# A hybrid decoder step: 48 instead of 32 prompt units inside the sample loop, all scores of the next unit first, and SyncE as the one issuer of value transfers

## What is computed

```python
mod = silu(c) @ w_ada + b_ada                  # (9, 6144): shift, scale, gate, twice; one row per sequence
h = x * (1 + scale1) + shift1
qa, ka, va, qb, kb, vb = split(h @ w_in)       # 6 column groups of 512; rope on the q and k groups
# mixer A: 8 heads of 64; keys at distance 0..128, 0..512 by 4, 0..2048 by 16, three softmaxes mixed
# mixer B: 4 heads, two q/k maps each: (softmax(q1 k1) - lambda softmax(q2 k2)) v, then an RMS norm
x = layer_norm(alpha * x + gate1 * (concat(oa, ob) @ w_o))
x = layer_norm(alpha * x + gate2 * conv_ffn(x * (1 + scale2) + shift2))
# outputs also: the samples' key and value windows moved on by 8 rows (HBM to HBM copies, 4080 KB each, 16 of them)
```

## Time and profile before

| | |
|---|---|
| median of three runs | 1229.12 us (1226.54 to 1235.38) |
| profiled run: its own time | 1233.46 us |
| profiled run: span | 1231.5 us |
| busy in the span: PE, DVE, POOL, ACT | 1052.7, 839.2, 357.9, 269.5 us |
| bytes moved by the DMA queues | 276.54 MB, mean 225 GB/s |

### The profile page before, as it was taken

The page is one execution under the profiler, slowest core; times in us unless marked ns, Lnnn a source line. Parts: engine busy times, 40 slices in busy tenths (PEclk is TensorE's granted clock), DMA queues, the critical chain, the costliest instruction groups (busy, mean ns, idle before and its releaser), DMA issues.

```text
span 1231.5 us, 23995 instructions
## 1 busy us (share of the span) xinstructions
PE 1052.7 (85%) x9389; PEld 854.0 (69%) x9389; DVE 839.2 (68%) x1513; ACT 269.5 (22%) x580; POOL 357.9 (29%) x379
## 2 busy tenths in 40 slices
PE   5599999999578677677776996999999999999994
PEld 3377777666455555455555775999999999677772
DVE  1657457167676767667659467567676687998958
ACT  0310010132132223322242104332233222100002
POOL 2333233100000000000016005456565665433323
PEclk9699999999888889778786997999999999999997
DMA  8959895596899999999990215475567731413102
GB/s 303 399 171 327 300 353 174 187 331 220 279 351 344 316 367 322 360 313 343 333 322 1 64 53 195 143 265 207 205 244 274 264 105 69 149 58 106 70 17 77
DMA packets 112549, 276.54 MB, mean 225 GB/s; under 512 B 9608, under 2 KB 33174, under 8 KB 108837
## 3 DMA queue, kind: packets, MB, share of 16 engines
q1 hardware_dynamic: 99125, 250.82, 58.6%
q10 hardware_dynamic: 13312, 24.19, 5.5%
HBM read 264.60 MB, written 76.69 MB: 277 GB/s over the span
## 4 chain that ended last, share of the span: by engine, by line
PE 60%; DVE 18%; DMA 7%; SPq 7%; issue 4%; POOL 2%; ACT 2%; ACTq 0%; DVEq 0%; POOLq 0%; PEldq 0%
PE wide L1576 16%; PE wide L1578 15%; PE wide L1577 15%; DVE ring L1151 3%; PE wide L1650 2%; DMA ring<-in_cache_k 2%; DMA ring<-in_w_ada 2%; PE wide L1639 2%; PE wide L1701 2%; PE wide L1732 2%; DVE ring_r L1083 2%; SPq L598 2%; SPq L433 1%; PE wide L1525 1%; DMA ring<-in_w_down 1%
## 5 line engine op out<-in xcount | busy, mean ns | idle before, releaser
L747 POOL TENSOR_TENSOR ring_r<-ring,ring_r 128x1024 fp32r<-128x1024 f32 x70 | 184.9, 2650 | 271.4 <-DVE ring_r L1043 204.5
L1576 PE MATMUL wide<-x_sb_r,ring_r 128*128 128x288 f32 x704 | 211.4, 300 | 8.2 <-DVE ht_r L1065 5.1
L1577 PE MATMUL wide<-ht_r,ring_r 128*128 128x288 f32 x704 | 209.3, 297 | 0.0
L1578 PE MATMUL wide<-x_sb_r,ring_r 128*128 128x288 f32 x704 | 208.7, 296 | 0.0
L1578 PE MATMUL wide<-ring_r,ht_r 128*128 128x512 f32 (+1 forms) x400 | 158.2, 395 | 0.0
L1151 DVE STREAM_TRANSPOSE ring<-ring 128x512 f32<-128x512 f32 x208 | 129.2, 673 | 20.8 <-DMA ring<-in_cache_k 19.0
L1576 PEld LDWEIGHTS wide<-x_sb_r,ring_r 128*128 128x128 f32 x704 | 133.3, 189 | 11.7 <-issue 11.2
L1578 PEld LDWEIGHTS wide<-x_sb_r,ring_r 128*128 128x128 f32 x704 | 134.2, 191 | 0.0
L1577 PEld LDWEIGHTS wide<-ht_r,ring_r 128*128 128x128 f32 x704 | 133.8, 190 | 0.0
L1576 PE MATMUL wide<-ring_r,x_sb_r 128*128 128x512 f32 (+1 forms) x240 | 97.0, 404 | 10.5 <-DVE ht_r L1065 8.5
L1701 PE MATMUL wide<-ring,x_sb 128*32 128x128 f32 (+1 forms) x1792 | 69.3, 305 | 40.4 <-DVE ring L1151 40.3
(11 more groups left out here) (226 smaller groups left out, 1900.0 us busy)
## 6 DMA issues: line engine op xcount, KB each, us to landing
ring<-in_cache_k SPq DMA_DIRECT2D x128, 256.0 KB
out_wks<-in_cache_win_k SPq DMA_DIRECT2D x8, 4080.0 KB, 19.0
out_wvs<-in_cache_win_v SPq DMA_DIRECT2D x8, 4080.0 KB, 25.3
ring<-in_w_ada SPq DMA_DIRECT2D x12, 2048.0 KB, 10.0
ring<-in_w_up SPq DMA_DIRECT2D x22, 1024.0 KB, 7.6
ring<-in_cache_win_k SPq DMA_DIRECT2D x16, 1024.0 KB
ring<-in_w_in SPq DMA_DIRECT2D x6, 2048.0 KB, 18.4
room<-in_cache_v ACTq DMA_DIRECT2D x32, 256.0 KB
```

The costliest lines, as they stand in the source:

```text
L747: nc.gpsimd.tensor_tensor(rest, w, high.bitcast(F32), ALU.subtract).then_inc(wl_rest, 1)
L1576: nc.tensor.matmul(out, left[0], right[0], start=first, stop=False)
L1577: nc.tensor.matmul(out, left[0], right[1], start=False, stop=False)
L1578: return nc.tensor.matmul(out, left[1], right[0], start=False, stop=last)
```

## The change

- **Modulation moved.** `ada` 4 to 11 leave the prompt stage. They run between the projection units, at the units in `LATE_UNIT`, through one 2 MB buffer of their own (`late`), loaded one ahead by SP (`load_late`), which waits until the chunk before has been multiplied.
- **Window copies** of the first four samples are issued one at a time after the units in `COPY_UNIT`, not in pairs.
- **Prompt units.** `NU` is 16: heads 0 to 3 of mixer A stay in the prompt stage, the other 48 units go into the sample loop, three per step (`PER = 3`, `prompt_step`).
- **Queries** lie packed two heads to a tile (`qt`) rather than padded with zeros (`qtp`): the 4 MB memset on POOL goes, ACT copies each tile with one instruction instead of two, and the score product contracts 64 rows instead of 128.
- **Order on PE in a step.** All groups of step `w + 1` are scored first, then its new rows (into bank 7, not 4), then all groups of step `w` are weighed.
- **Issuing.** `values_by_act` is always false: SP issues all value groups, in the order keys (w, 0), keys (w, 1), values (w-1, 0), keys (w, 2), values (w-1, 1), keys (w, 3), values (w-1, 2 and 3), new keys of w, new values of w-1. ACT issues only mixer A's key tails (`load_key_tail`), behind its exponentials of the step.
- Buffers are laid out anew; new keys and new values have one buffer each instead of two.

The core of the diff:

```diff
+LATE_UNIT = {4: 3, 5: 6, 6: 10, 7: 13, 8: 16, 9: 20, 10: 23, 11: 26}
+COPY_UNIT = {1: (0, "k"), 4: (0, "v"), 8: (1, "k"), 11: (1, "v"), 14: (2, "k"), 18: (2, "v"), 21: (3, "k"), 24: (3, "v")}
...
-        NU = 32
+        NU = 16
         pb = pa[NU:]
+        PER = len(pb) // (2 * DB)
...
         def values_by_act(w, g):
-            return w < len(sa) and w > 0 and (g < 2 if sa[w][0] else g == 1)
+            return False
+        def load_key_tail(eng, w):
+            G = NG[w] + 2
+            ks = G % NK
+            if G >= NK:
+                eng.wait_ge(kg_t, G - NK + 1)
+            win_k = flat_k[0][sa[w][1]].rearrange("(g r) h d -> g r (h d)", r=16)
+            for i in range(4):
+                eng.dma_start(kraw[ks][32 * i:32 * i + 32, 0:2, :], win_k[96:128, 8 + i:16:4, :]).then_inc(kg_in[ks], 16)
...
+            def load_late(ch):
+                if ch > 4:
+                    sp.wait_ge(ada_mm, ch)
+                src = a["w_ada"][0].rearrange("(k p) n -> p k n", p=P)
+                sp.dma_start(late, src[:, :, CH * ch:CH * ch + CH]).then_inc(late_in, 16)
...
+            load_keys(0, 0)
+            load_keys(0, 1)
+            sp.wait_ge(w_used, CHUNK_AT[("in", 5)] + 1)
+            sp.wait_ge(ada_mm, 12)
+            load_key_tail(sp, 0)
+            for w in range(1, len(sa) + 1):
+                here = len(groups[sa[w][0]]) if w < len(sa) else 0
+                if here:
+                    load_keys(w, 0)
+                    load_keys(w, 1)
+                load_values(sp, w - 1, 0)
+                if here == 4:
+                    load_keys(w, 2)
+                load_values(sp, w - 1, 1)
+                if here == 4:
+                    load_keys(w, 3)
+                for g in range(2, len(groups[sa[w - 1][0]])):
+                    load_values(sp, w - 1, g)
+                if here:
+                    sp.wait_ge(kn_t, w)
+                    load_new_keys(sp, w)
                 if w >= 2:
-                    sp.wait_ge(kn_t, w - 1)
                     sp.wait_ge(sa_pv, w - 1)
-                    load_new(sp, w)
+                    load_new_values(sp, w - 1)
...
+                if w + 1 < len(sa) and sa[w + 1][0] == 0:
+                    load_key_tail(act, w + 1)
...
-                for g in range(4):
-                    if g < len(nxt):
-                        score_group(w + 1, g)
-                    if g == 0:
-                        pe.wait_ge(sa_pt, 2 * w + 2)
-                        pe.wait_ge(sa_ph, w + 1)
-                    if g < len(groups[m]):
-                        weigh_group(w, g)
-                    if g == 2:
-                        turn_b(2 * w)
-                        scores_b(2 * w + 1)
+                for g in range(len(nxt)):
+                    score_group(w + 1, g)
+                    if g == 1:
+                        prompt_step(PER * w + 1)
+                if nxt:
+                    score_new(w + 1)
+                else:
+                    prompt_step(PER * w + 1)
+                pe.wait_ge(sa_pt, 2 * w + 2)
+                pe.wait_ge(sa_ph, w + 1)
+                for g in range(len(groups[m])):
+                    weigh_group(w, g)
+                    if g == 1:
+                        if nxt:
+                            pe.wait_ge(sa_min, w + 2)
+                        prompt_step(PER * w + 2)
```

More of the change, by code:

```diff
@@ L144, in build, with mod_s @@
         lam4 = part(room, 3584, 256).rearrange("p (n d) -> p n d", n=4)
[L146 to L150, removed]
+        mod_early = ht[:, :, :].rearrange("p k t -> p (k t)")[:, 6 * NT:6 * NT + 2 * CH].rearrange("p (b n) -> p b n", b=2)
+        mod_late = mix[:, 2048:2048 + 2 * CH].rearrange("p (b n) -> p b n", b=2)
+        def mod_s(ch):
+            return (mod_early if ch < 4 else mod_late)[:, ch % 2, :]
+        late = part(room, 12288, KT_D * CH).rearrange("p (k n) -> p k n", k=KT_D)
+        qt = part(room, 0, 4096).rearrange("p (f t) -> p f t", f=8)
+        kt = part(room, 4096, 4096).rearrange("p (f t) -> p f t", f=8)
+        vp = part(room, 8192, 4096).rearrange("p (m t d) -> p t m d", t=TP, m=2)
         tmp_a = part(room, 16384, 1024).rearrange("p (b n) -> p b n", b=2)
@@ L276, in build @@
         vg_in = [sem(f"v_group_loaded_{i}") for i in range(NV)]
-        new_in = [sem(f"new_rows_loaded_{i}") for i in range(2)]
+        kn_in, vn_in = sem("new_keys_loaded"), sem("new_values_loaded")
         new_zero, qbd_zero = sem("new_zeroed"), sem("queries_zeroed")
@@ L560, in _ @@
                 if t == TP:
[L561 to L565, removed]
-            sp.wait_ge(page_in, 16)
[L569 to L601, removed]
@@ new lines, in _, with load_keys @@
+                    if s < 4:
+                        load_chunk(6 + s)
+                for ch, at in LATE_UNIT.items():
+                    if at == n and ch < 11:
+                        load_late(ch + 1)
+                if n in COPY_UNIT:
+                    i, which = COPY_UNIT[n]
+                    move_window(i, (("cache_win_k", "wks") if which == "k" else ("cache_win_v", "wvs"),))
+            sp.wait_ge(page_in, 16)
+            sp.wait_ge(w_used, CHUNK_AT[("in", 4)] + 1)
+            def load_keys(w, g):
+                m, b = sa[w]
+                G = NG[w] + g
+                ks = G % NK
+                if G >= NK:
+                    sp.wait_ge(kg_t, G - NK + 1)
+                if m == 0:
+                    win_k = flat_k[0][b].rearrange("(g r) h d -> g r (h d)", r=16)
+                    sp.dma_start(kraw[ks][:, :, :], win_k[:, 4 * g:4 * g + 4, :]).then_inc(kg_in[ks], 64)
+                else:
+                    for t, pg in enumerate(page_numbers(sp, b, g)):
+                        sp.dma_start(kraw[ks][:, t, :], flat_k[1][bass.ds(pg, 1)].rearrange("a p h d -> (a p) (h d)"))\
+                            .then_inc(kg_in[ks], 16)
@@ L721, in _ @@
             pool.wait_ge(w_used, CHUNK_AT[("in", 5)] + 1)
+            for i, place in enumerate((kn, ktn)):
+                nc.gpsimd.memset(place, 0.0).then_inc(new_zero, 1)
+                pool.wait_ge(new_zero, i + 2)
             nc.gpsimd.memset(qbd, 0.0).then_inc(qbd_zero, 1)
@@ L731, in _ @@
                 last.then_inc(q_bd, 1)
[L732 to L737, removed]
             def rest_of_piece(q):
@@ L1106, in _ @@
             jobs += [(5 * c - 1.4, "split", c) for c in range(1, 6)]
+            jobs += [(n - 0.5, "late_rows", ch) for ch, n in LATE_UNIT.items()]
+            jobs += [(n + 0.55, "late_sum", ch) for ch, n in LATE_UNIT.items()]
             dve.wait_ge(rope_in, 16)
             for _, what, n in sorted(jobs):
+                if what == "late_rows":
+                    ada_rows(n)
+                    continue
+                if what == "late_sum":
+                    ada_sum(n)
+                    continue
                 if what == "split":
@@ L1517, in ada_rows @@
             def ada_rows(ch):
-                n = CHUNK_AT[("ada", ch)]
-                landed(n)
+                if ch < 4:
+                    landed(CHUNK_AT[("ada", ch)])
+                else:
+                    pe.wait_ge(late_in, 16 * (ch - 3))
+                w = slot(SLOT_OF[CHUNK_AT[("ada", ch)]]) if ch < 4 else late
                 if ch:
@@ L1581, in _ @@
             for n in range(len(units) + 3):
+                for c, at in LATE_UNIT.items():
+                    if at == n - 1:
+                        ada_sum(c)
+                    if at == n:
+                        ada_rows(c)
                 if n < len(units):
```

201 lines of the change are left out of this document (105 added, 96 removed).

## The result

The changed kernel takes **1291.49 us** (median of 4 runs, 1289.89 to 1293.09); the kernel before took 1232.25 us beside it (4 runs, 1226.54 to 1236.00). The ratio is 1.050, 95% interval 1.047 to 1.054. The forecast was 1262 us: the direction and the loop came as expected, the prompt stage did not, and the loss is nearly twice the size. The profiled runs are 1289.9 and 1233.5 us, 56.4 apart.

The account below looks back on a forecast made before the run. PE bounds projection and prompt stage; DMA engines and SP's issuing (37 of 40.1 us a pair) nearly tie in the loop. From 1233.5 us, -18 + 59 - 8 = +33 gives 1266, less 4 to the median: 1262 us, range 1226 to 1293.

Parts of the forecast that it names:

- Modulation into the projection: Projection: eight moved chunks add 23 us of PE work, plus 3 us of PE stalls (bounds 0 and 10).
- second rival: Projection: `late` chunks land behind the copies, PE stalls 10 to 20 us more; 1275 us, chance 0.10.
- The prompt stage: Prompt stage: four units without their chunk take 5.9 us; first keys come earlier, front -18 us (-21 to -11).
- the edits at 0: Projection: zero-padded queries, memset, one copy instead of two and relaid buffers, taken to change the time by 0.
- The loop, by SP: Sample loop: SP's issuing takes 47 us per pair of steps, 373 us in all; +59 us (+33 to +83).
- first rival: Sample loop: transfers stay the limit, pair stays at 40.1 us; 1211 us, chance 0.16.
- Waits at the new order: Sample loop: SP holding values until earlier groups are weighed costs about 1 us of wait a pair.
- third rival: Sample loop: SP waits 5 or more us a pair for weighing or turning; 1302 us, chance 0.08.
- End: Loop's end: backlog of queued transfers gone, 10.5 us instead of 18.4 after SP's last value issue; -8 us (-8 to -4).
- 16 more units inside: Sample loop: 16 more prompt units add 29 us on PE, costing nothing while the issuer sets the pace.

Follow-up runs that it names:

- e4: Changed kernel with prompt score products over all 128 rows instead of 64, adding two heads' scores together: 1272.95 us, ratio 1.035.
- e5: Kernel before with score products over 64 rows, modulation products left in the prompt stage: 1241.04 us, ratio 1.012.
- e6: Changed kernel with page numbers written into the program instead of looked up by SP, same number and shape of transfers: 1245.50 us, ratio 1.014.
- e12: Changed kernel with ACT issuing the first new rows after its sixth prompt-stage exponential, not ahead of the first: 1273.24 us, ratio 1.036; profiled run 1288.51 us.
- e1: Kernel before with SP issuing all value groups, in the old order: 1294.85 us, ratio 1.054.
- e2: Changed kernel with value groups 2 and 3 of each mixer B step issued by ACT again: 1253.22 us, ratio 1.020.
- e8: Changed kernel with modulation chunks 8 to 11 back between prompt units and ACT issuing value groups 2 and 3 of mixer B steps: 1229.87 us, ratio 1.000.
- e9: e8 with ACT issuing value groups 1 to 3 of mixer B steps and each step's new value rows: 1276.88 us, ratio 1.040.
- e3: Changed kernel plus eight unused modulation-shaped products after every fourth unit of the prompt stage: 1283.38 us, ratio 1.043.

## Why the prediction was right in kind and short in size

- **Modulation into the projection: right.** +26 forecast, +27.6 measured, with PE waiting 4.9 us for the one late chunk (3 taken, 10 the bound). The second rival (1275) did not occur.
- **The prompt stage: the step that failed.** It was "a period without its chunk is 8.77 - 2.86 = 5.9 us, 1.47 us a unit". Four units took 294.06 - 281.44 = 12.6 us, so the way from the stage's start to the first keys took 47.5 us where 26.9 were forecast. That is 20.6 of the 23.9 us by which the profiled run came out over its forecast of 1266 (projection 1.6, loop 2.5, end -0.9 are the rest, with rounding). The subtraction assumed that the rest of the period keeps its speed when a third of PE's work in it is taken out. Every row of before that it used stood at a clock of 1.00. With 128-row scores (e4) the subtraction holds to the tenth; with 64-row scores, which the forecast listed among the edits at 0, it does not. e4's stage takes 27.0 us and the changed kernel's 47.5. Of the 20.5 between them about 4 are the scores themselves (four periods at 1.0, from e5 and e6), and the other 16 or 17 go with the lower clock. That the clock was lower is read from the rows; why the same instructions of PE ran at either level (e6, e12) stays open.
- **The loop, by SP: right.** 47 us a pair and 373 us forecast, 47.5 and 375.5 measured; one issuer's time is shown as the bound from both sides (e1, e2, e6). The first rival (1211, transfers stay the limit) had the DMA share of 0.99 for it; it is refuted, for e1 alone costs 65 us. The 37 us that the sum started from were taken from one pair of 40.1 us, a little shorter than the mean of 40.9; that hardly moves the sum.
- **Waits at the new order: right.** 1 us a pair forecast; 11.8 us in the 305 us, 1.8 a pair. The third rival's 5 us a pair did not occur in the changed kernel; they came in e8, where SP no longer sets the pace.
- **End: right.** -8 forecast, -8.9 measured.
- **16 more units inside: right** as covered by SP. e2 shows them at 40.5 us a pair, so they do not lengthen the pair there either.

## What to carry to other kernels

Count the issuer as an engine of its own: here two limits lay within 10% of each other (transfers at 0.99, SP at 37 of 40 us), and one line that moves issues turned them over (e1). An issue moved to a computing engine delayed what stood behind it there (e9). When work is subtracted from a stage, the rest of it may not keep its price, for the clock in the rows was granted with that work in place. So ask of each stage what the engine would still be doing, and keep a variant that leaves part of the removed work in place.

## What was not expected of the hardware

PE shows 40.00 busy us in 40 and yet a granted clock of 0.50, and adding products to that same stage brought 1.00 back (e3). A record of a busy PE is no evidence that its clock is up. e6 went back to 1.00 within the stage with PE's instructions unchanged. The same program (e12) gave runs 15 us apart with one kind at a mean clock of 0.897 and the other at 0.905 and more, so a single profile of such a kernel can mislead. Half the rows made a 512-wide score product slower, 641 against 594 ns, not faster.

The rule of the Trainium skill that the prediction names ("DMA: Bandwidth & Descriptors", section "Issuing engines are not separate DMA queues"), that the time to initiate a transfer is usually small relative to the transfer, was put to the test by e1. With value pages of 256 KB (0.78 us each at 338 GB/s) and 0.60 us of issue plus page reading for each, leaving all values to one issuer cost 5.4%.
